# Layer A's windowed attention: key-major value products, 64-row scores and projections woven in

## The reference

```python
q, k, v, g = split(u @ w_in)              # 16 q heads, 4 k/v heads, 16 gate heads, 64 wide
q, k = axial_rope(q), axial_rope(k)       # latent tokens only
for each block of 128 queries:            # 8 latent blocks
    s = [q.k over blocks b-1, b, b+1 with |i-j| <= 128] + [q.k over 256 context keys] + [sink]
    o = softmax(s * 64**-0.5) @ [v, v_ctx]
o_ctx = softmax([qc.kc, sink]) @ vc       # 2 context blocks
y = (o * silu(g)) @ w_out                 # for latents and for context
h = layer_norm(alpha * h + gate * y)
```

## Time and profile before

| stretch | us | PE busy | DVE busy | ACT busy |
|---|---|---|---|---|
| profiled execution (device time 3304.69) | 3302.9 | 94% | 61% | 39% |
| layer A, 1555 to 2205 | 650.0 | 610.0 | 364.1 | 277.1 |
| one turn of layer A | 72.06 | 68.4 | 40.3 | 31.8 |
| one turn of fox | 77.03 | 75.4 | 45.9 | 36.8 |
| one turn of layer B | 95.67 | 93.7 | 54.3 | 44.9 |

### The profile page before, as it was taken

One profiled execution on the slowest core, in us unless ns is written; L12 is line 12 of the kernel. 1 busy time (PEld: TensorE's weight loads), 2 busy tenths in 40 slices (PEclk: granted clock), 3 DMA queues, 4 the chain that ended last, 5 costly groups with the idle time before them and its releaser, 6 DMA issues.

```text
span 3302.9 us, 48157 instructions
## 1 busy us (share of the span) xinstructions
PE 3099.5 (94%) x17866; PEld 2556.4 (77%) x17866; DVE 2000.0 (61%) x3834; ACT 1299.8 (39%) x2326; POOL 759.5 (23%) x324
## 2 busy tenths in 40 slices
PE   8999999999999989997999999999899999999976
PEld 5888888777777767875888888887577787777764
DVE  5676776565656558856655455455755555655555
ACT  4534444444444430122443444340344444454412
POOL 2222333222222214542111111113122121111221
PEclk9999999999999999997999999999999999999998
DMA  3111111111111157511201000152201111100241
GB/s 115 45 39 45 45 64 39 65 52 53 66 59 61 58 200 270 186 57 57 71 30 45 31 26 30 46 201 111 85 26 50 44 50 44 47 34 33 86 149 64
DMA packets 64834, 237.85 MB, mean 72 GB/s; under 512 B 7008, under 2 KB 10080, under 8 KB 63600
## 3 DMA queue, kind: packets, MB, share of 16 engines
q1 hardware_dynamic: 31680, 115.91, 10.1%
q10 hardware_dynamic: 32944, 119.10, 9.6%
HBM read 185.11 MB, written 49.87 MB: 71 GB/s over the span
## 4 chain that ended last, share of the span: by engine, by line
PE 81%; DVE 9%; ACT 4%; issue 3%; DVEq 2%; DMA 1%; ACTq 0%; SPq 0%; POOL 0%; POOLq 0%
PE ps L184 22%; PE ps L1293 21%; PE ps L353 9%; PE ps L1357 5%; PE ps L1323 4%; PE ps L1339 4%; PE ps L880 3%; PE ps L475 3%; PE ps L857 2%; PE ps L129 2%; DVE fox_l L1444 1%; PE ps L841 1%; PE ps L842 1%; ACT nb_l L1373 1%; ACT nb_pt_hi L1382 1%
## 5 line engine op out<-in xcount | busy, mean ns | idle before, releaser
L205 POOL TENSOR_TENSOR w_hi<-raw,small 128x1024 fp32r<-128x1024 f32 x160 | 333.8, 2086 | 2458.2 <-PE ps L1293 1101.0
L207 POOL TENSOR_TENSOR w_lo<-raw,w_hi 128x1024 fp32r<-128x1024 f32 x160 | 425.5, 2659 | 22.8
L1293 PE MATMUL ps<-nb_u_hi,w_hi 128*128 128x512 f32 (+1 forms) x640 | 250.2, 391 | 8.2 <-DVE nb_u_lo L2139 4.1
L1293 PE MATMUL ps<-nb_u_hi,w_lo 128*128 128x512 f32 (+1 forms) x640 | 246.8, 386 | 0.0
L1293 PE MATMUL ps<-nb_u_lo,w_hi 128*128 128x512 f32 (+1 forms) x640 | 245.7, 384 | 0.0
L1455 DVE TENSOR_TENSOR nb_pt_lo<-ps,nb_pt_hi 128x512 fp32r<-128x512 f32 x208 | 143.9, 692 | 144.4 <-ACT nb_pt_hi L1382 143.9
L353 PE MATMUL ps<-u_hi,w_hi 128*128 128x512 f32 x528 | 213.8, 405 | 8.6 <-DVE u_lo L267 3.8
L353 PE MATMUL ps<-u_hi,w_lo 128*128 128x512 f32 x528 | 209.8, 397 | 0.0
L353 PE MATMUL ps<-u_lo,w_hi 128*128 128x512 f32 x528 | 209.6, 397 | 0.0
L1293 PE MATMUL ps<-u_hi,w_lo 128*128 128x512 f32 x512 | 208.9, 408 | 0.0
L1293 PE MATMUL ps<-u_hi,w_hi 128*128 128x512 f32 x512 | 208.3, 407 | 0.0
(11 more groups left out here) (356 smaller groups left out, 7972.4 us busy)
## 6 DMA issues: line engine op xcount, KB each, us to landing
raw<-in_w_stream SPq DMA_DIRECT2D x160, 512.0 KB, 3.6
h_sb<-in_w_ada ACTq DMA_DIRECT2D x16, 1024.0 KB, 5.6
nf_b<-nf_rows ACTq DMA_DIRECT2D x16, 512.0 KB, 4.4
nb_bias<-in_rel_bias ACTq DMA_DIRECT2D x16, 448.0 KB, 3.9
y_parts<-wa_y_hi ACTq DMA_DIRECT2D x8, 640.0 KB, 3.0
y_parts<-wa_y_lo ACTq DMA_DIRECT2D x8, 640.0 KB, 4.1
la_out_yh<-y_parts SPq DMA_DIRECT2D x8, 640.0 KB, 9.6
la_out_yl<-y_parts SPq DMA_DIRECT2D x8, 640.0 KB, 10.7
```

The source lines that it names most:

```text
L205: pool.tensor_tensor(w_hi[:, s, :], raw[:, s, :], zero, ALU.add)
L207: pool.tensor_tensor(w_lo[:, s, :], raw[:, s, :], w_hi[:, s, :].bitcast(F32), ALU.subtract).then_inc(w_ready, 1)
L1293: mm = pe.matmul(ps[:, b:b + ch["n"]], w(slot, k), u[:, k, ch["c0"]:ch["c0"] + ch["n"]], start=k == 0 and p == 0, stop=k == KT - 1 and p == 2)
```

## The change

Layer A's attention becomes a subclass of `Flow`, class `Window`, in the place of `Attention`, which goes. Its score blocks are in five segments of two blocks (the fifth is the context), V weights are [v_hi | v_lo] of a k/v head that both query heads share, so a group of four transposes is one value product of 512 columns for hi and one for lo. All 20 units are planned in one order of work, in two halves of four turns; the projections lie between attention steps by a cost for each step, the next turn's rotated Q is made by chunks of 512, and scores of the next turn begin in this one. The last 16 groups of the last turn get no projections. The stored y goes out in two parts, latents and context.

```diff
+WA_ORDER = [("Q", 0), ("K", 0), ("V", 0), ("Q", 1), ("G", 0), ("Q", 2), ("G", 1), ("Q", 3), ("G", 2), ("K", 1),
+            ("Q", 4), ("G", 3), ("V", 1), ("Q", 5), ("G", 4), ("Q", 6), ("G", 5), ("Q", 7), ("G", 6), ("G", 7)]
-        class Attention:
...
+        class Window(Flow):
+            rotated = True
+            spills = 2
...
+                first_parts = [(0, k[0], None), (2, k[1], k[0]), (24, q[0], k[1]), (26, k[2], k[2]), (28, q[1], q[0]),
+                               (50, q[2], q[1]), (51, None, q[2])]
...
+                    row, s_at = scores[order[0]], 44 if its[0] == 0 else 30
...
+                        if seg == segs - 2:
+                            pending = [s for o in order[n + 1:n + 3] for s in scores[o]]
+                            at_slot = (0, 2, 5, 7, 9)
+                        elif seg == segs - 1:
+                            pending = []
+                        else:
+                            pending, at_slot = nxt[0] if nxt else [], (0, 3, 5, 7)
+                        for i, (items, adds) in enumerate(rows):
+                            mine = [[s for s, p in zip(pending, at_slot) if p == 2 * i + half] for half in range(2)]
+                            cost = 1.2 + 0.14 * len(items) + sum(0.4 + 2 * s["blk"]["pieces"][s["piece"]]["n"] / 1000
+                                                                 for s in mine[0] + mine[1])
...
+                    until = len(plans) if its[-1] < PAIRS - 1 else len(plans) - 16
...
+            def rotate(self, dve, ch, part):
+                x, cols = self.stage(ch)
+                if part == 0:
+                    dve.wait_ge(*ch["raw"])
+                    if ch["c0"] < T:
+                        dve.drain()
+                        dve.stream_shuffle(self.shuffled[:], x, [(i + 16) % 32 for i in range(32)])
+                        dve.drain()
+                        dve.tensor_tensor(x, x, rope[:, 0, cols], ALU.mult)
+                elif ch["c0"] < T:
+                    dve.tensor_tensor(self.shuffled[:], self.shuffled[:], rope[:, 1, cols], ALU.mult)
+                    dve.drain()
+                    dve.tensor_tensor(x, x, self.shuffled[:], ALU.add).then_inc(self.roped, 1)
...
+        wa = Window("wa", [[window_block(b), window_block(b + 1)] for b in (0, 2, 6, 4, 8)], True, False, fox)
...
+        wa.plan(wa_units(0, 2), [(wa_units(2, 3), wa_units(3, V1), range(4)),
+                                 (wa_units(V1, V1 + 1), wa_units(V1 + 1, len(WA_ORDER)), range(4, 8))])
```

The first four chunks (Q and K of turn 0, 1024 tokens) are projected beside each other, tile by tile, as `mod_a` makes the tiles. The residual is now stored unscaled, in the loop of the gate products, and `layer_a` multiplies it by the rows, which are saved to DRAM between the two parts of `mod_a`; the rows lie in banks 0 and 1:

```diff
@@ ple_act (loop)
+                    act.dma_start(h_dram[ds(i * 2 + m, 1), :, 0:T].rearrange("a p t -> (a p) t"),
+                                  h_sb[:, ds(i * 2 + m, 1), :].rearrange("p a t -> p (a t)")).then_inc(h_stored, 16)
@@ norm4_pe
-            spread_rows(pe, T, diag4, 6, 2)
+            spread_rows(pe, T, diag4, 0, 2)
-        def scale_h3(dve):
...
+        def store_rows4(act):
+            act.wait_ge(mod_a.made, KT)
+            act.wait_ge(h_stored, 16 * (KT + 1))
+            nc.scalar.copy(wa.silu[:, 0:T], bank(0, 2)).then_inc(rows4_saved, 1)
+            act.drain()
+            act.dma_start(rows4_dram, wa.silu[:, 0:T]).then_inc(rows4_stored, 16)
@@ Layer.dve
-                    if l == 1:
-                        dve.wait_ge(rows_loaded, 16)
-                        dve.scalar_tensor_tensor(self.res[:, m, :], self.res[:, m, :], vecs[:, V_LNG + k:V_LNG + k + 1],
-                                                 self.rows[:], ALU.mult, ALU.mult)
+                    dve.wait_ge(rows_loaded, 16 * (l + 1))
+                    v = (V_FINAL, V_LNG)[l] + k
+                    dve.scalar_tensor_tensor(self.res[:, m, 0:T], self.res[:, m, 0:T], vecs[:, v:v + 1],
+                                             self.gains, ALU.mult, ALU.mult)
+                    dve.drain()
```

More of the change, by code:

```diff
@@ L995, in __init__ @@
                 self.s_bank, self.t_bank, self.o_bank, self.p_bank = banks
-                self.NU = 2 * sum(len(s) for s in segments)
+                self.NU, self.per_turn = 2 * sum(len(s) for s in segments), len(segments)
                 def signal(what):
@@ L2167, in window_block @@
-            chunks = [(c * P, P, lo + c) for c in range(hi - lo)] + [(n + c * P, P, 8 + c) for c in range(2)]
-            return {"b": b, "width": n + C + 1, "first": CH - n, "runs": runs, "chunks": chunks, "lat": n}
+            lo, hi = (max(b - 1, 0), min(b + 2, 8)) if b < 8 else (0, 0)
+            n = (hi - lo) * P
+            lat, context = (0, lo * P, n), (n, T, C)
+            if n + C <= CH:
+                pieces = [{"l0": 0, "n": n + C, "runs": ([lat] if n else []) + [context]}]
+            else:
+                pieces = [{"l0": 0, "n": n, "runs": [lat]}, {"l0": n, "n": C, "runs": [(0, T, C)]}]
@@ L2193, in wa_pe @@
[L2193 to L2212 removed]
+        T_SPANS = [(0, CH), (CH, CH)]
@@ new lines, in build_program, with wa_units, before @@
+        TC_SPANS = T_SPANS + [(T, C)]
+        def wa_units(*kinds):
+            return [(kind, it, U_A + n, TC_SPANS) for n, (kind, it) in enumerate(WA_ORDER)][kinds[0]:kinds[1]]
+        V1 = WA_ORDER.index(("V", 1))
+        wa.plan(wa_units(0, 2), [(wa_units(2, 3), wa_units(3, V1), range(4)),
+                                 (wa_units(V1, V1 + 1), wa_units(V1 + 1, len(WA_ORDER)), range(4, 8))])
+        def wa_pe(pe):
+            def before(ch):
+                return [mod_a.ctx_ready()] if ch["seq"] == 4 else []
+            flow = wa.projections(pe, mod_a.hi, mod_a.lo, mod_a.ready, before)
+            wa.pe(pe, wa.lead, flow, lambda s: [])
+            for steps in wa.turns:
+                wa.pe(pe, steps, flow, lambda s: [])
@@ new lines, in wa_dve, with masks @@
+        def wa_dve(dve):
+            def masks(it, s, hd):
+                b, n = s["blk"]["b"], s["blk"]["lat"]
+                win = consts[:, K_WIN:K_WIN + 3 * P + C]
+                if b == 7:
+                    return [(0, n, win[:, 0:n]), (n, C, win[:, 3 * P:])]
+                if n + C <= CH:
+                    return [(0, n + C, win[:, 3 * P - n:])]
+                return [(0, n, win[:, 0:n])] if s["piece"] == 0 else [(n, C, win[:, 3 * P:])]
+            dve.wait_ge(a_loaded, 32)
+            dve.tensor_scalar(wa.nsink[:], wa.nsink[:], -1.0, None, ALU.mult)
+            dve.drain()
+            dve.wait_ge(h_stored, 16 * (KT + 1))
+            wa.dve(dve, wa.lead, None, masks, lambda dve, ch: None, None)
+            dve.wait_ge(rows4_saved, 1)
+            for steps in wa.turns:
+                wa.dve(dve, steps, lambda it, hd: wa.nsink[:, 2 * it + hd:2 * it + hd + 1], masks,
+                       lambda dve, ch: None, None)
@@ L2320, in build_program @@
         NEAR_W = 10 * GRID_W
[L2321 removed]
+        nb = Flow("nb", [[near_block(b), near_block(b + 1)] for b in (0, 2, 6, 4)], False, True, wa)
         nb.allocate_first(ph7, T, TC)
```

740 lines of the change are left out of this document (368 added, 372 removed).

## The result

The kernel before takes 3303.62 us and the changed one 3312.51 us (medians of 13 runs each; 3300.2 to 3310.05 and 3307.84 to 3316.36). The ratio is 1.0025, with a 95% interval of 1.0016 to 1.0033: slower by a quarter of a per cent, where 3263 was forecast. The profiled execution of the changed kernel took 3314.26 us.

The account below looks back on a forecast made before the run. TensorE was taken to set the pace. Last value product at 1602 + 271.6 + 24.3 + 256.1 + 8 = 2162; 17.4 later the last head's tile, 2179.4 against 2222.6, 43 us earlier: 3263 on the median's basis, range 3238 to 3298.

Parts of the forecast that it names:

- The prices: TensorE's costs from the old trace: 384 keys of scores 0.94 us, 256 keys 0.77, four transposes 0.44.
- factor of 1.03: Applied to layer A's woven stretches, since fox measured 77.03 us against 74.8 priced, layer B 95.67 against 92.8.
- density: Layer A's turns: VectorE busy 54 of 70 us, 77%, costing 1 us a turn, 8 in all.
- VectorE nearly the bound: Rival for layer A: VectorE can be kept busy only 74%, turns 73 instead of 70.1, +23: 3286; chance 0.16.
- Lead: From VectorE's start of `mod_a` at 1535.2 to the first group at 1602, bounds 1597 and 1612.
- First three turns: Part of layer A's first half, where 9 units and four turns were to take 263.7 x 1.03 = 271.6 us.
- Fourth turn and border: End of the first half, then the border: V again 18.3 us and a stall of 6, bounds 0 and 12.
- Turns 5 to 7 and the last turn: Layer A's second half: 7 units and four turns, 243.1 us, and 13 for the last 16 groups.
- Tail: From the last value product to the last head's tile in `layer_a`: 17.4 us, start at 2179.4.
- the parts costed at nothing: Stores of h, rows' product, copy and store, sinks' load, two-part store, scratch size: covered by other work, 0 us.
- Rival 1: VectorE in layer A can be kept busy only 74% of the time, +23: 3286; chance 0.16.
- The weighed rule: GpSimd's splits lock out VectorE's SBUF-only operations: 2 us of VectorE a turn, off the path; 31 if all wait.

Follow-up runs that it names:

- e14: Changed kernel without layer A's rotation and silu, and with VectorE's low part of the probabilities for 64 of 512 columns only; 3272.36 us, ratio 0.9901.
- e6: Changed kernel with VectorE writing the sinks' column before it waits for the score, not behind the pass; 3309.02 us, ratio 1.0016.
- e3: Changed kernel without the rotation of layer A's Q and K; 3288.96 us, ratio 0.9962.
- e13: Changed kernel with VectorE's low part of the probabilities worked out for 64 of 512 columns only, behind the first segment; 3292.83 us, ratio 0.9968.
- e7: Changed kernel with the last 10 groups without projections instead of the last 16; 3304.60 us, ratio 1.0000.
- e2: Changed kernel with the last G unit of projections spread over the last turn's 22 groups instead of ending 16 groups before the end; 3325.86 us, ratio 1.0074.
- e11_two: Changed kernel with the sinks' column ahead of the score's wait and the last 10 groups without projections instead of 16; 3297.35 us, ratio 0.9983.

## Why the prediction was wrong

**The prices held.** In the new order, at full clock, 384 keys of scores cost TensorE 0.92 us (from 2039.8), where 0.94 was taken, 256 keys 0.74 (0.77), a value product of 512 columns 0.24 (0.23) and four transposes 0.46 (0.44). With much of the load gone (e14) three turns took 3.7% more than the list with its factor of 1.03.

**The step that failed** is the term "density": 1 us a turn, 8 in all, for VectorE at over 70%. Between the first and the last value product the changed kernel takes 597.9 us and e14, which leaves out rotation, most of the low parts and silu, 565.7: 32 us, 4 a turn, where the sum had 8. Some 22 of the 32 are waits, the rest is time in which TensorE was busy with the same work at a lower clock (25.6 us of clock lost, and 17.0 in e14). And e6 shows that the cost hangs not on VectorE's share alone, but also on what stands in the chain that releases TensorE. The prediction itself said that no row stood behind this term. VectorE's load was right (50 to 54 us), its share nearly right (70 to 76%), and the rival "VectorE nearly the bound" has the first half's turns (73.9 for 73) but not the time: 3286, and 3312.5 was measured. It had 0.16, because "against" I counted the 2 us that a turn of layer B loses at 57%. The runs show that this can't be carried over to 73%.

**The steps in order.** The last head's tile starts at 2230.7, forecast 2179.4, so 51.3 are to be found (2222.7 before). Of them 24 are the density term's, by e14; the rest is spread over the steps, and of those parts only the tail is traced to single operations.
- *Lead:* transposes of the first group at 1605.3 against 1602: +3.3, inside its bounds. The score waited until 1592.4, forecast 1589.
- *First group's start:* its first value product came at 1611.1, 5.8 us behind its transposes: +5.8. TensorE was busy all the while, at a clock of 0.71, with eleven projections, a score and more transposes, 4.4 us by the list, which the sum had in its turns. So only 1.4 is lost here, and the turns lose 4.4 more than the next lines say.
- *First three turns:* 221.6 against 3 x 67.9 + 3 = 206.7: +14.9. e14 wins 10.4 of the 17.9 over the list without density, 3.5 a turn where 1 was taken. The other 7.5 stay with VectorE at 53%, waits for exponentials before all (7.7 us in these turns).
- *Fourth turn and border:* 100.4 against 67.9 + 24.3 + 1 = 93.2: +7.2, with three waits of 1.8 to 3.1 us for low parts (1892.8 to 1901.9) as K's copies pass VectorE and ScalarE. It is the rotation that costs here: without it (e3) the window takes 94.5, without low parts (e13) 100.5.
- *Turns 5 to 7 and the last turn:* 209.7 against 204.3 (7 units over 72 groups), +5.4, and 66.3 against 55.8, +10.5. But the planner laid out the projections otherwise than the sum. By the lengths of the matmuls in these windows turns 5 to 7 hold 79.2 us of them at the list's price, not 89.1, and the last turn a whole unit, 13.9 and not 8.1. With that the forecasts are 194.1 and 61.8, and the misses 15.6 (5.2 a turn, as in the first half) and 4.5. In the last turn the clock is 0.85, where the earlier trace rows, from which the idle time was taken, had 0.98 and 1.00. The same turn took 63.0 at 0.89 in e7 and 54.5 at 0.97 in e2.
- *Tail:* 21.7 against 17.4: +4.3. Silu (2208.60), gate, split and issues of the latents stood ahead of the last segment's; I had counted the context's part alone.

These sum to 51.4. From the last head's tile to layer B's first product it is 147.7 us, and was 148.6, so the output stage did not get longer; the parts costed at nothing (stores of h, the rows' product, their copy) show no wait of TensorE that wasn't there before. Two slips in the sum change nothing: V's start adds up to 1571.1, not 1571.6, and the tail's terms to 17.3.

**What the range missed.** Rival 1 was worked out alone, as +23, and each other term at its middle. But VectorE's load, the low clock behind many of the waits, and the border all rise together: TensorE's waits, 53 us before in this stage, were 81 after, and the lost clock doubled. A range for cases that go together has to add their upper ends.

**The weighed rule.** Two of VectorE's groups between 1620 and 2140, by form (count, busy us, mean ns), and two operations beside GpSimd's:

```profile
L2243 DVE COPY wa_l<-wa_nsink 128x2 f32<-128x2 f32 x69 | 21.2, 307 | 0.0
L2298 DVE TENSOR_TENSOR wa_q_lo<-wa_rq,wa_q_hi 128x512 fp32r<-128x512 f32 x14 | 11.4, 815 | 0.0
...
1634.01 1.89 POOL L207 TENSOR_TENSOR w_hi<-raw,small 128x1024 fp32r<-128x1024 f32 x1 [28.70 <-PE ps L1033]
1636.04 2.39 POOL L209 TENSOR_TENSOR w_lo<-raw,w_hi 128x1024 fp32r<-128x1024 f32 x1
...
1634.58 1.34 DVE L2243 COPY wa_l<-wa_nsink 128x2 f32<-128x2 f32 x1
1636.44 2.54 DVE L2298 TENSOR_TENSOR wa_q_lo<-wa_rq,wa_q_hi 128x512 fp32r<-128x512 f32 x1
```

A copy takes 0.17 us (at 1759.47) and such a product 0.69. Nine of the 69 copies took 0.75 to 2.07 us, and each of the nine ended within 0.05 us of the end of a split on GpSimd. In all, twenty operations of VectorE that read and write SBUF alone were stretched like this, every one beside a split, by 26 us together: 3.6 a turn, where I said 2. The Trainium skill ("SBUF — State Buffer", section "SBUF: two separate sides") lets VectorE wait out a whole GpSimd instruction; single operations waited out what was left of one, up to 2 us, but it was not 31 us a turn. What I had not seen is that the sinks' copies are among the stalled ones, with one SBUF input, and a link of the chain that transposes and scores wait for: the score that waited 2.12 us at 2130.1 stood behind such a copy (1.10 from 2128.92). e6 takes that link off the chain.

## What to carry to other kernels

An engine that is 75% busy, in order and in bursts, is not free room: here it cost 4 us a turn, which the turns with 57 and 60% before had not shown. Taking a microsecond of work from it gave TensorE back a third at first and less later, and taking one short operation off the chain gave as much, over three turns, as 18 to 26 us less work. Before trading TensorE's work for VectorE's, look up the highest share at which such a woven order has run, and price what lies above it; then take links out of the chain that releases TensorE rather than issue things earlier, which here only moved the waits. Where a planner leaves groups uncovered, find which transfer it waits out (here 22 us of loads, with 38 us given to it) before filling them.

## What the runs showed of the hardware

The clock fell behind short waits: 0.91 over the 20 us from 1695 with one wait of 1.76 us in it; 0.50 from 2135 to 2145, behind one of 2.12 us at 2130.1 and in a stretch without projections. The next projection starts at 2144.87, and from 2145 to 2155 the clock is 0.99. It did not fall behind every wait: of the 25 waits of 1 us and more between 1611 and 2209 in the changed kernel, the 5 us behind twelve were below full clock, and behind thirteen, up to 2.01 us at 1892.8, they were not. Up to the last head's tile this stage lost 21 us of clock before, 41 after, and 27 in e11_two (summed over windows of 10 us, the clock being read to a hundredth). How much of the loss any one wait causes was not measured by itself and stays open.
